# Expert weights in 16 KB pieces, with gate and up in two stages

## The reference

```
x2     = rmsnorm(h, norm_ffn)                      # (320, 2048)
g_idx  = argmax(x2 @ w_router_group + b)           # 4 groups
e_prob = softmax(x2 @ w_router_expert[g_idx] + b)  # 8 experts in the group, top 2 used
y      = sum over both: gate * (silu(x2 @ w_gate[e]) * (x2 @ w_up[e])) @ w_down[e]
out    = rmsnorm(h + y, norm_final)
```

## Time and profile before

| | |
|---|---|
| median of 3 runs | 1612.42 us |
| profiled execution, span | 1613.5 us |
| TensorE matmul busy | 1272.8 us, 79% |
| VectorE, ScalarE busy | 393.7 us, 378.5 us |
| weight queue (q1) | 470.86 MB, 73.3% of 16 engines' span |
| granted TensorE clock, mean | 0.896 |

### The profile page before, as it was taken

The page is one execution under the profiler, slowest core; times in us unless marked ns, Lnnn a source line. Parts: engine busy times, 40 slices in busy tenths (PEclk is TensorE's granted clock), DMA queues, the critical chain, the costliest instruction groups (busy, mean ns, idle before and its releaser), DMA issues.

```text
span 1613.5 us, 19649 instructions
## 1 busy us (share of the span) xinstructions
PE 1272.8 (79%) x7570; PEld 655.1 (41%) x7571; DVE 393.7 (24%) x737; ACT 378.5 (23%) x643; POOL 31.9 (2%) x41
## 2 busy tenths in 40 slices
PE   5999999999899996677677677568678666766765
PEld 4999998566566641221122122122122112212212
DVE  6354443245554330120120120120113012012013
ACT  5333322143433221112112112112120111211213
POOL 1001000001000000000000000000000000000000
PEclk9999999999899988888878889879897888988987
DMA  9444540123433389999989999999976998999993
GB/s 322 140 144 154 157 138 33 37 81 107 129 125 106 130 338 420 420 374 420 421 363 422 421 373 420 421 406 390 420 293 247 420 421 366 421 420 384 422 420 139
DMA packets 110801, 475.38 MB, mean 295 GB/s; under 512 B 14156, under 2 KB 51136, under 8 KB 60304
## 3 DMA queue, kind: packets, MB, share of 16 engines
q1 hardware_dynamic: 109776, 470.86, 73.3%
q0 software_dynamic: 832, 2.48, 0.4%
q10 hardware_dynamic: 64, 0.02, 0.0%
HBM read 469.96 MB, written 3.38 MB: 293 GB/s over the span
## 4 chain that ended last, share of the span: by engine, by line
PE 61%; DMA 26%; issue 7%; DVE 2%; ACT 1%; SPq 1%; ACTq 0%; DVEq 0%
DMA ring<-in_w_up 14%; PE ps L843 12%; DMA ring<-in_w_down 11%; PE ps L871 7%; PE ps L574 5%; PE ps L575 5%; PE ps L576 5%; PE ps L858 5%; PE ps L822 3%; PE ps L746 2%; PE ps L635 2%; PE ps L662 2%; PE ps L755 2%; PE ps L748 2%; PE ps L747 2%
## 5 line engine op out<-in xcount | busy, mean ns | idle before, releaser
L843 PE MATMUL ps<-ring,mix 128*32 128x512 f32 x2112 | 335.6, 772 | 242.9 <-issue 131.6
L843 PEld LDWEIGHTS ps<-ring,mix 128*32 128x32 f32 x2112 | 75.3, 131 | 495.7 <-issue 322.0
L1533 DVE TENSOR_TENSOR mix<-mix,ps 128x128 f32<-128x128 f32 x33 | 9.5, 288 | 765.5 <-ACT mix L1166 765.5
L1163 ACT COPY mix<-ps 128x512 f32<-128x512 f32 x33 | 35.5, 1076 | 616.0 <-PE ps L843 616.0
L574 PE MATMUL ps<-xT_hi,w_hi 128*128 128x320 f32 (+1 forms) x528 | 165.8, 314 | 3.9 <-DVE work L1258 3.9
L575 PE MATMUL ps<-xT_lo,w_hi 128*128 128x320 f32 (+1 forms) x528 | 164.8, 312 | 0.0
L576 PE MATMUL ps<-xT_hi,w_lo 128*128 128x320 f32 (+1 forms) x528 | 164.6, 312 | 0.0
L858 PE MATMUL ps<-ring,mix 128*32 128x512 f32 x1056 | 122.3, 596 | 29.4 <-DVE mix L1533 17.6
L871 PE MATMUL ps<-mix 128*128 128x512 f32 (+1 forms) x192 | 99.6, 678 | 23.9 <-ACT mix L1171 23.1
L822 PE MATMUL ps<-r,work 128*32 128x512 f32 (+1 forms) x816 | 107.9, 616 | 0.4 <-DVE work L1516 0.2
L1272 DVE TENSOR_TENSOR w_lo<-ring,w_hi 128x1024 fp32r<-128x1024 f32 (+1 forms) x66 | 76.8, 1205 | 117.3 <-ACT w_hi L978 117.3
(11 more groups left out here) (259 smaller groups left out, 1117.4 us busy)
## 6 DMA issues: line engine op xcount, KB each, us to landing
ring<-in_w_gate SPq DMA_DIRECT2D x128, 1024.0 KB, 20.7
ring<-in_w_up SPq DMA_DIRECT2D x128, 1024.0 KB, 22.8
ring<-in_w_down SPq DMA_DIRECT2D x128, 1024.0 KB, 23.6
ring<-in_w_in SPq DMA_DIRECT2D x32, 1024.0 KB, 8.1
ring<-in_w_o SPq DMA_DIRECT2D x16, 1024.0 KB, 6.2
hreg<-in_x_prompt SPq DMA_DIRECT2D x4, 1024.0 KB, 6.1
ring<-in_w_uq SPq DMA_DIRECT2D x4, 768.0 KB, 4.9
ring<-in_w_uv SPq DMA_DIRECT2D x2, 1024.0 KB, 5.9
```

What stands on the lines that cost most here:

```text
L843: last = pe.matmul(ps[r:r + B, 2, :], x[:, c + o, s, :], w[:, m, c + o, :], start=s == 0 and c == 0, stop=s == 3 and c == 2)
```

## The change

- A slot among 0 to 3 now holds a half of one matrix: slot 0 gate's first half, slot 1 up's first half, slots 2 and 3 the second halves. A half is 8 of each partition's 16 rows, which lie side by side in memory: 16 KB in one piece. Slots 4 and 5 hold half of down each, 16 KB in one piece too. Each slot is one DMA of 2 MB.
- `gate_up` works in two stages of 16 matmuls, each after both its slots have landed; `weights_used` counts four stages per expert instead of six slots. `extra_used` has four semaphores instead of six.
- The partition `p` now holds rows 16p to 16p+15 of gate and up (before: four rows of each quarter), so `xn` keeps its columns in another order.
- The router transposes read the residual rows `xtile` instead of `xn`, and wait for the residual add alone. The gain goes into the router weights instead, by one VectorE product over 128 x 576, with the gain loaded as 16 more rows of the parameter block. The router weights come in two DMAs instead of eight.

```diff
         def expert_slot(i, gate_w, up_w, down_w):
             if i < 4:
-                s = ring[:, i, :].rearrange("p (m c n) -> p m c n", m=2, c=4)
-                return [(s[:, m], w[512 * i:512 * i + 512, :].rearrange("(p c) n -> p c n", c=4))
-                        for m, w in enumerate((gate_w, up_w))]
-            s = ring[:, i, :].rearrange("p (c n) -> p c n", c=2)
-            v = down_w.rearrange("(p c) n -> p c n", c=4)
-            return [(s[:, c], v[:, 2 * (i - 4) + c, :]) for c in range(2)]
+                v = (gate_w, up_w)[i % 2].rearrange("(p c) n -> p (c n)", c=KC)
+                return ring[:, i, :], v[:, SLOT * (i // 2):SLOT * (i // 2 + 1)]
+            v = down_w.rearrange("(p c) n -> p (c n)", c=4)
+            return ring[:, i, :], v[:, SLOT * (i - 4):SLOT * (i - 3)]
...
                 for i in range(SLOTS):
-                    sp.wait_ge(weights_used, e * SLOTS + (i + 1 - SLOTS))
-                    sp.wait_ge(extra_used[i], used)
+                    stage = (0, 0, 1, 1, 2, 3)[i]
+                    sp.wait_ge(weights_used, e * 4 + (stage + 1 - 4))
+                    sp.wait_ge(extra_used[stage], used)
                     w = [a[k][0, bass.ds(e, 1)].rearrange("a b c -> (a b) c") for k in ("w_gate", "w_up", "w_down")]
-                    for dst, src in expert_slot(i, *w):
-                        sp.dma_start(dst, src).then_inc(slot_full[i], 16)
+                    dst, src = expert_slot(i, *w)
+                    sp.dma_start(dst, src).then_inc(slot_full[i], 16)
...
             def router_transpose(n, i):
                 tn = TILES[i][1]
-                pe.wait_ge(hg_ready, 3 * n + i + 1)
+                pe.wait_ge(drained["dve"], drain_count[f"wo{n}_{i}"])
                 b = claim(pe, f"rt{n}_{i}")
                 for c in range(4):
-                    last = pe.transpose(b[:, c * tn:(c + 1) * tn], xn[0:tn, i, 4 * n + c, :], ident[0:tn, 0:tn])
+                    f = 512 * n + P * c
+                    last = pe.transpose(b[:, c * tn:(c + 1) * tn], xtile[0:tn, i, f:f + P], ident[0:tn, 0:tn])
...
-            def gate_up(x, s):
-                w = ring[:, s, :].rearrange("p (m c n) -> p m c n", m=2, c=4)
-                for c in (0, 2):
+            def gate_up(x, half):
+                w = ring[:, 2 * half:2 * half + 2, :].rearrange("p m (c n) -> p m c n", c=8)
+                for c in (0, 2, 4, 6):
                     for m in range(2):
                         for o in range(2):
                             r = B * (2 * m + o)
-                            last = pe.matmul(ps[r:r + B, 2, :], x[:, c + o, s, :], w[:, m, c + o, :],
-                                             start=s == 0 and c == 0, stop=s == 3 and c == 2)
+                            k = 8 * half + c + o
+                            last = pe.matmul(ps[r:r + B, 2, :], x[:, k % 4, k // 4, :], w[:, m, c + o, :],
+                                             start=half == 0 and c == 0, stop=half == 1 and c == 6)
...
-                    for s in range(4):
-                        pe.wait_ge(slot_full[s], e * 32 + expert_count(s))
-                        gate_up(xg, s).then_inc(weights_used, 1)
+                    for half in range(2):
+                        for s in (2 * half, 2 * half + 1):
+                            pe.wait_ge(slot_full[s], e * 16 + expert_count(s))
+                        gate_up(xg, half).then_inc(weights_used, 1)
...
             link(dve.memset(work[:, 1024:2560], 0.0))
+            dve.wait_ge(s_router, 64)
+            dve.tensor_tensor(wr, wr, par[:, P_FFN:P_FFN + KC].unsqueeze(2).to_broadcast([P, KC, G + NE]), ALU.mult).then_inc(wr_scaled, 1)
...
-                    dve.tensor_tensor(xn[0:tn, i, 4 * n:4 * n + 4, :].rearrange("t c q -> t q c"),
-                                      h.rearrange("t (q c) -> t q c", c=4), gain[0:tn, f].rearrange("t (q c) -> t q c", c=4),
+                    dve.tensor_tensor(xn[0:tn, i, :, 32 * n:32 * n + 32].rearrange("t c q -> t q c"),
+                                      h.rearrange("t (q c) -> t q c", c=KC), gain[0:tn, f].rearrange("t (q c) -> t q c", c=KC),
                                       ALU.mult).then_inc(hg_ready, 1)
```

More of the change, by code:

```diff
@@ L63 @@
 C_ALL = C_SIN + T
-P_MIX, P_Q, P_KV, P_CONV, P_AO, P_CO, P_ST = 0, 16, 20, 24, 48, 56, 64
-P_ALL = 80
+P_MIX, P_Q, P_KV, P_CONV, P_AO, P_CO, P_ST, P_FFN = 0, 16, 20, 24, 48, 56, 64, 80
+P_ALL = 96
 W_CQ, W_KV, W_KR, W_CONV, W_UV, W_PAIR, W_O = 0, 2, 4, 5, 17, 18, 22
@@ L294, in trunk_layer_kernel @@
         hg_ready, h_squared, logits_full = sem("hg_ready"), sem("h_squared"), sem("logits_full")
+        wr_scaled = sem("wr_scaled")
         hot_ready, route_in, route_act, route_pe = sem("hot_ready"), sem("route_in"), sem("route_act"), sem("route_pe")
@@ L307, in trunk_layer_kernel @@
         x_ready, x_hcopied, x_folded = sem("x_ready"), sem("x_hcopied"), sem("x_folded")
-        x_silu, x_hT, x_ycopied, extra_used = sem("x_silu"), sem("x_hT"), sem("x_ycopied"), [sem(f"extra_used{s}") for s in range(SLOTS)]
+        x_silu, x_hT, x_ycopied, extra_used = sem("x_silu"), sem("x_hT"), sem("x_ycopied"), [sem(f"extra_used{s}") for s in range(4)]
         x_gtfull, x_gtcopied, x_full, x_added = sem("x_gtfull"), sem("x_gtcopied"), sem("x_full"), sem("x_added")
@@ L342, in expert_count @@
         def expert_count(s):
-            return 32 * (1 + sum(1 for k in range(W_END) if slot_of_item(k) == s))
+            return 16 + 32 * sum(1 for k in range(W_END) if slot_of_item(k) == s)
         def wslot(n):
@@ L404, in expert_slot @@
             if i < 4:
-                s = ring[:, i, :].rearrange("p (m c n) -> p m c n", m=2, c=4)
-                return [(s[:, m], w[512 * i:512 * i + 512, :].rearrange("(p c) n -> p c n", c=4))
-                        for m, w in enumerate((gate_w, up_w))]
-            s = ring[:, i, :].rearrange("p (c n) -> p c n", c=2)
-            v = down_w.rearrange("(p c) n -> p c n", c=4)
-            return [(s[:, c], v[:, 2 * (i - 4) + c, :]) for c in range(2)]
+                v = (gate_w, up_w)[i % 2].rearrange("(p c) n -> p (c n)", c=KC)
+                return ring[:, i, :], v[:, SLOT * (i // 2):SLOT * (i // 2 + 1)]
+            v = down_w.rearrange("(p c) n -> p (c n)", c=4)
+            return ring[:, i, :], v[:, SLOT * (i - 4):SLOT * (i - 3)]
         def late_loads(sp):
             sp.wait_ge(psum_full, full(f"K{H - 1}_1"))
[L416 to L420, removed]
+            sp.dma_start(wr[:, :, 0:G], a["w_router_group"][0].rearrange("(c p) e -> p c e", p=P)).then_inc(s_router, 16)
+            sp.dma_start(wr[:, :, G:G + NE],
+                         a["w_router_expert"][0].rearrange("(c p) g e -> p c (g e)", p=P)).then_inc(s_router, 16)
             sp.dma_start(brow[:, 0:G], a["b_router_group"].to_broadcast([P, G])).then_inc(s_router, 16)
@@ L466, in _ @@
                 wait_slot_free(sp, used_by[holder[i]] if i < SPLIT_SLOTS - 1 else "wo3_2")
-                for dst, src in expert_slot(i, a["w_gate"][0, 0], a["w_up"][0, 0], a["w_down"][0, 0]):
-                    sp.dma_start(dst, src).then_inc(slot_full[i], 16)
+                dst, src = expert_slot(i, a["w_gate"][0, 0], a["w_up"][0, 0], a["w_down"][0, 0])
+                sp.dma_start(dst, src).then_inc(slot_full[i], 16)
             sp.wait_ge(routed, 4)
@@ L547, in _ @@
             pe.wait_ge(s_const, 16)
-            pe.wait_ge(s_par, 16 * 4)
+            pe.wait_ge(s_par, 16 * 5)
             pe.wait_ge(s_par_pool, 16 * 3)
@@ L788, in _ @@
                 if n == 0:
-                    pe.wait_ge(s_router, 160)
+                    pe.wait_ge(wr_scaled, 1)
                     pe.wait_ge(rooted, 2)
@@ L887, in extra_blocks @@
                         pe.wait_ge(x_ready, x)
-                        for s in range(4):
-                            gate_up(xx, s).then_inc(extra_used[s], 1)
+                        for half in range(2):
+                            gate_up(xx, half).then_inc(extra_used[half], 1)
                         pe.wait_ge(x_hcopied, x)
@@ L894, in extra_blocks @@
                         for s in (4, 5):
-                            down(s).then_inc(extra_used[s], 1)
+                            down(s).then_inc(extra_used[s - 2], 1)
                         pe.wait_ge(x_ycopied, x)
@@ L900, in extra_blocks @@
                         combine(lambda n: (gTx[B * n:B * (n + 1), :], yx[B * n:B * (n + 1), :]), x_full, x_added, lambda v: x * 12 + v)
-            for s in range(SLOTS):
+            for s in range(4):
                 pe.sem_inc(extra_used[s], 1)
@@ L952, in _ @@
             loads = ((P_MIX, a["norm_mix"], 16), (P_Q, a["norm_q"], 4), (P_KV, a["norm_kv"], 4),
-                     (P_AO, a["norm_attn_out"], 8))
+                     (P_AO, a["norm_attn_out"], 8), (P_FFN, a["norm_ffn"], 16))
             for first, src, n in loads:
@@ L1184, in extra_blocks @@
                         act.copy(gTx, ps[:, 0, 0:T]).then_inc(x_gtcopied, 1)
```

(8 more changed lines are left out.)

## The result

The changed kernel takes 1639.02 us (median of 4 runs, 1637.44 to 1646.56) against 1611.3 beside it: ratio 1.018, 95% interval 1.0153 to 1.0207. It is slower by 28 us. The forecast was 1637 and slower.

The account below looks back on a forecast made before the run. The expert stage was taken as bound by the weight stream, whose queue runs dry once per group. Terms 17.6 + 15.2 - 8.6 = +24.2 us on the median 1612.42 gave 1637 us, range 1622 to 1648.

Parts of the forecast that it names:

- First return of slots: Expert stage, start of each group: first slots come back 1.7 to 2.9 us later with the queue dry, +17.6 us.
- Tail: Last expert of a group, last gate and up landing to end of down: 13.9 us instead of 11.88, +15.2 us.
- The low end of this term: Last expert's 16 matmuls take 3.84 us at full clock, so the whole loss there is only +4.3 us.
- Pieces: Weight stream, where it sets the cycle: 16 KB pieces gain 1.2% of 717 us, -8.6 us.
- the line: Straight line through engine times of 2 and 8 KB pieces: 614 ns for 16 KB against 629, 2.4%.
- Router part: Before the expert stage: changed transposes, gain product and router loads are hidden or behind TensorE, 0 us.
- this sign of being wrong: Anything before the expert stage's start at 588 us moving by more than 1 us would show the prediction wrong.
- The restarts of undisturbed groups: Weight stream restarts in groups without an extra block: 126 to 129 us apart, where before 123.5 to 125.6.
- Rival A: First pause behind the combine grows 2.6 us in six groups, as fetches wait behind pieces; 1652 us, chance 0.25.
- Rival D: Weight DMAs: 16 KB pieces are cut into the old ones, leaving only the coarser stages; 1645 us, chance 0.08.
- B: Faster: stream pieces lose their fixed cost (-34 us), last expert's matmuls keep the clock (+4.3); 1600 us, chance 0.17.
- C: No change: stream gains 2.4% (-17), last expert's matmuls hidden behind down data, against +17.6; 1613 us, chance 0.08.

Follow-up runs that it names:

- late return: Kernel before, but SP waits for slots 0 and 1 until slot 1 is used, and for 2 and 3 until slot 3 is used: 1633.27 us, ratio 1.0125.
- the down weights alone: Kernel before with only the down weights in 16 KB pieces, one DMA of 2 MB per slot, fine stages as before: ratio 1.0001.
- late start: Kernel before, but TensorE waits for both slots of a half before its first matmul; slots given back one by one: 1627.96 us, ratio 1.0095.

## Why the prediction was right

**First return of slots: +17.6 forecast, +16.0 in the profile, +16.7 alone.** The price was read from the old return of slot 1, with the same matmuls behind it. The first issue came 4.8 to 6.3 us after the start of gate and up. The two kernels with the same stages and 8 KB pieces have +18.6 and +15.4 here, so 1.6 us off is within what executions vary by.

**Tail: +15.2 forecast, +14.3.** The 5.2 us for 16 matmuls were 3.64 to 6.6. They go with the granted clock: 1.00 in the fourth group, which lost nothing (11.9 us), and 0.55 to 0.72 in the seven others, each time after a wait for weights of 3.3 to 4.0 us. The length of the wait alone doesn't tell which it will be: behind one of 3.93 us the clock was 1.00, behind one of 4.02 it was 0.68. The second and the fourth group (columns of the windows as above):

```profile
802.33:807.30 4.97, 4.97 (x36) 1.40 (x40) 0.00 (x0) 0.00 (x0) 0.00 (x0) 0.72 1.01 429
...
1059.63:1063.40 3.77, 3.77 (x36) 1.19 (x40) 0.00 (x0) 0.07 (x1) 0.00 (x0) 1.00 0.99 422
```

The low end of this term was too high: it put the 16 matmuls at 3.84 us at full clock and the tail at +4.3, where the fourth group shows 3.64 and no loss.

**Pieces: -8.6 forecast, -10.5.** 616 ns per 16 KB, where the line through 2 and 8 KB said 614. I had halved the line's gain because the 2 KB stretch isn't saturated; in engine time the line was nearer (2.1% gained, the line said 2.4). The stretch itself gained 1.6%, as the bytes moved in 50 us did (20.96 and 21.28 MB), which lies between the 1.2% taken and the line. The ceiling of 435 GB/s that the Trainium skill gives ("DMA: Bandwidth & Descriptors", Where 436 GB/s comes from) was not reached: 429 is the highest of the page's slices.

**Router part: 0 forecast; 0.12% measured, with an interval that holds 0.** The sentence that I would be wrong if anything before 588 us moved by more than 1 us was too tight: that point moved by 1.8 with no cause in the change, since two kernels without any edit there have it at 585.6 and 585.7. By the letter this sign of being wrong came true. The restarts of undisturbed groups, forecast 126 to 129 us apart, were 126.0 to 129.5.

**Not forecast: +6.1 us between down and the next gate and up.** Some 2.4 us of it are the first pause (4.74 to 5.24 against 4.50 to 4.83). The rest is spread over seven places. It isn't the price of the change: the same stretch adds up to 209.3 us with the router part alone, 207.1 with late return alone, 211.5 with the down weights alone, and 204.4 in the changed kernel with 8 KB pieces, where before has 204.6. So it varies by as much without the stages or the pieces; what moves it stays open.

**How near the number was, and why.** The three forecast terms, +24.2, came to +19.8 in the profile. That the span still grew by 22.5 is the 6.1 that was not forecast, less 1.8 in front and 1.6 at the end, none of which belongs to the change as far as the runs show. The mechanism and each term's size were right to 2 us; that 1637 and 1639 lie 2 apart is in part luck, since the interval of the ratio alone spans 25 to 33 us.

**Rival A fell.** The first pause behind the combine was to grow by 2.6 us with the pieces. It reads 4.74, 5.04, 5.24, 5.04, 4.74 and 4.95, a mean of 0.3 over before; the second pause didn't grow (2.65 to 3.62 against 3.56 to 4.23). Beside the dry queue of the sixth group:

```profile
1246.32 2.66 issue
```

So beside a running stream the pause keeps nearly its length when the pieces double, and a wait for a fixed number of pieces is excluded. That the pause is an instruction fetch is argued, not shown: the profile has it as time in which TensorE waited for nothing that it records. The Trainium skill's rule ("DMA: Bandwidth & Descriptors", Queues, rings and completion order) that an engine drains a whole packet of descriptors from one ring first does not show here as a wait that grows with the piece; whether a packet holds fewer of the longer pieces no run here can tell. Rival D fell because the weights came in 1299 pieces of 16 KB and because 8 KB pieces in the same stages are slower, B and C because the queue gained 1.6% and not 3.1%, and because the tail didn't keep the clock.

## What to carry to other kernels

In a stream with a ring of buffers, a coarser stage is paid where the stream runs dry, and there twice: at the first buffer returned and behind the last one landed. Here that was 38 us with a dry queue in every group and 8 without. Find those places first: here the combine between two groups made all of them but those at the extra block and at the ends. Moving it gave 1.3% by itself and turned a loss of 1.8% into a gain of 1.8%. A small gain per piece can only be judged in a kernel where the stream is the bound all the time.

## What was unexpected of the hardware

- Two pieces of 8 KB took 629 ns of engine time and one of 16 KB 616. The size of the DMA (1 or 2 MB) made no difference with the same pieces (1650.2 and 1649.0 us).
- The first pause behind the combine, at the loop's end, was 4.4 to 4.9 us beside a running stream of 8 KB pieces, in all kernels that keep the combine in its old place, and 4.7 to 5.2 beside one of 16 KB; beside a dry queue it was 1.9 to 2.7.
- Where TensorE waits for two slots at a time, the mean granted clock was lower: in the profiled executions 0.896 in the kernel before and with late return alone, 0.882 with late start alone and 0.887 in the changed kernel. With the combine moved the gap is smaller: 0.889 to 0.896 in six runs with two stages and 8 KB pieces, 0.895 to 0.904 in six of the fine form.
- The start of the first gate and up lay between 585.6 and 587.8 us in the profiled executions of three kernels that are alike up to there (the kernel before, late return, late start).
